# Key scores of a retention layer in three single-precision passes, placed inside the second product

## The reference, cut to what matters

```python
q = rotate_pairs(q, cos, sin)
k = rotate_pairs(k, cos, sin) * (dk ** -0.5)
scores = jnp.einsum('bhid,bhjd->bhij', qc, kc) * inner_decay[None]
inner = jnp.einsum('bhij,bhje->bhie', scores, vc)
out = out * lax.rsqrt(jnp.mean(out * out, axis=-1, keepdims=True) + RMS_EPS)
return (jax.nn.silu(g) * out) @ w_out
```

## Time and profile before

| | |
|---|---|
| median of 3 runs | 1968.48 us (1968.37 to 1968.97) |
| profiled execution | 1968.52 us |
| its span, first to last instruction | 1966.7 us |
| granted PE clock, mean | 0.999 of full speed |
| PE busy | 1943.1 us (99%) |
| DVE busy | 1464.6 us (74%) |
| ACT busy | 891.1 us (45%) |

### The profile page before, as it was taken

The page is one execution under the profiler, slowest core; times in us unless marked ns, Lnnn a source line. Parts: engine busy times, 40 slices in busy tenths (PEclk is TensorE's granted clock), DMA queues, the critical chain, the costliest instruction groups (busy, mean ns, idle before and its releaser), DMA issues.

```text
span 1966.7 us, 23704 instructions
## 1 busy us (share of the span) xinstructions
PE 1943.1 (99%) x9192; PEld 1618.4 (82%) x9192; DVE 1464.6 (74%) x1858; ACT 891.1 (45%) x1244; POOL 219.7 (11%) x163
## 2 busy tenths in 40 slices
PE   8999999999999999999999999999999999999998
PEld 7788888888888888888888888888897898888886
DVE  7999953886767859999843999983369769989722
ACT  5554632352524435545621554562168435554510
POOL 0000011100000031000021000002145440000121
PEclk9999999999999999999999999999999999999999
DMA  4233132331313320422232242223222014222331
GB/s 172 86 120 138 48 115 76 143 134 43 134 43 134 113 102 2 152 104 86 89 102 79 99 155 98 86 89 103 83 90 82 1 55 160 86 86 101 103 99 62
DMA packets 76189, 189.53 MB, mean 96 GB/s; under 512 B 4144, under 2 KB 12336, under 8 KB 73008
## 3 DMA queue, kind: packets, MB, share of 16 engines
q1 hardware_dynamic: 76080, 188.04, 27.4%
HBM read 185.92 MB, written 2.10 MB: 96 GB/s over the span
## 4 chain that ended last, share of the span: by engine, by line
PE 87%; DVE 8%; issue 2%; ACT 2%; SPq 0%; DMA 0%; POOL 0%; DVEq 0%; ACTq 0%
PE bank L2444 12%; PE bank L2446 12%; PE bank L2445 12%; PE bank L2436 12%; PE bank L2437 12%; PE bank L2438 12%; PE bank L2663 3%; PE bank L2665 3%; PE bank L2664 3%; PE bank L2544 2%; DVE part_lo L1560 1%; DVE idx_scores L2245 1%; DVE best L2241 1%; PE bank L2674 1%; PE bank L2920 1%
## 5 line engine op out<-in xcount | busy, mean ns | idle before, releaser
L1022 ACT ACTIVATE part_hi<-quad_w 128x1024 fp32r<-128x1024 f32 x280 | 293.1, 1064 | 279.0 <-PE bank L2446 192.5
L1560 DVE TENSOR_TENSOR part_lo<-quad_w,part_hi 128x1024 fp32r<-128x1024 f32 x280 | 330.5, 1221 | 26.4 <-ACT part_hi L1022 26.1
L2436 PE MATMUL bank<-gated_hi,out_hi 128*128 128x512 f32 x704 | 275.0, 391 | 0.0
L2437 PE MATMUL bank<-gated_lo,out_hi 128*128 128x512 f32 x704 | 274.3, 390 | 0.0
L2438 PE MATMUL bank<-gated_hi,out_lo 128*128 128x512 f32 x704 | 274.3, 390 | 0.0
L2444 PE MATMUL bank<-part_hi,s_hi 128*128 128x512 f32 x640 | 252.7, 395 | 3.0 <-DVE part_lo L1560 3.0
L2446 PE MATMUL bank<-part_hi,s_lo 128*128 128x512 f32 x640 | 249.7, 390 | 0.0
L2445 PE MATMUL bank<-part_lo,s_hi 128*128 128x512 f32 x640 | 249.5, 390 | 0.0
L2444 PE MATMUL bank<-part_hi,xn_hi 128*128 128x512 f32 x608 | 237.7, 391 | 2.5 <-DVE part_lo L1560 2.4
L2446 PE MATMUL bank<-part_hi,xn_lo 128*128 128x512 f32 x608 | 236.9, 390 | 0.0
L2445 PE MATMUL bank<-part_lo,xn_hi 128*128 128x512 f32 x608 | 236.9, 390 | 0.0
(11 more groups left out here) (306 smaller groups left out, 3548.9 us busy)
## 6 DMA issues: line engine op xcount, KB each, us to landing
quad_w<-w_ffn_in SPq DMA_DIRECT2D x80, 1024.0 KB, 7.4
out_raw<-w_ffn_out SPq DMA_DIRECT2D x64, 704.0 KB, 4.1
quad_w<-w_ret_in SPq DMA_DIRECT2D x14, 1024.0 KB, 7.4
rest_raw<-w_ffn_in SPq DMA_DIRECT2D x32, 256.0 KB, 5.2
quad_w<-w_ret_in SPq DMA_DIRECT2D x16, 512.0 KB, 5.0
quad_w<-w_ret_out SPq DMA_DIRECT2D x8, 1024.0 KB, 5.2
w_raw<-w_dsa SPq DMA_DIRECT2D x7, 1024.0 KB, 4.9
x_res<-x_in SPq DMA_DIRECT2D x8, 256.0 KB, 6.1
```

The source lines that it names most:

```text
L1022: nc.scalar.activation(in_four(part_hi[part_slot(h)]), source, copy).then_inc(part_hi_made, 1)
L1560: nc.vector.tensor_tensor(in_four(part_lo[part_slot(h)]), source, in_four(part_hi[part_slot(h)]).bitcast(FP32), ALU.subtract)\
L2436: mm(to, w_hi_of[:, at:at + width], hi, start=start, stop=False)
L2437: mm(to, w_hi_of[:, at:at + width], lo, start=False, stop=False)
```

## The change

The rotated query and key of each head are split too. ACT makes `q_hi` and `k_hi` and DVE `q_lo` and `k_lo` (each one instruction of 128x1024), and the key scores become three fp32r matmuls for each of the 8 before, 24 in all. They move from between products 0 and 1 to between the halves of product 1. `k_rot` and its remainder now lie where `p1` is, and `k_hi` where `u2` is, so ACT's copy of product 0 to `p1` waits until all the key scores of the head are done (`act.wait_ge(scores_done, BLOCKS * (h + 1))`).

```diff
-    k_rot = at("k_rot", post + 12288, 2 * SEQ)
+    q_lo = at("q_lo", post + 8192, 2 * SEQ, FP32R)
+    q_hi = at("q_hi", post + 12288, 2 * SEQ, FP32R)
+    k_rot = at("k_rot", post, 2 * SEQ)
+    k_lo = at("k_lo", post, 2 * SEQ, FP32R)
+    k_hi = at("k_hi", post + 4096, 2 * SEQ, FP32R)
...
+                def rotated_hi(h, kind):
+
+                    n = "qk".index(kind)
+                    act.wait_ge(qk_rotated, 2 * h + n + 1)
+                    nc.scalar.activation((q_hi, k_hi)[n][:, :], (q_rot, k_rot)[n][:, :], copy)\
+                        .then_inc(qk_hi_made, 1)
...
                         split_ret("o", h - 1, 2)
+                        rotated_hi(h, "q")
                         split_ret("o", h - 1, 3)
+                        rotated_hi(h, "k")
                         product_hi(h, 0)
                     else:
                         product_hi(h, 0)
                         turned_hi(h - 1)
                     product_hi(h, 1)
+                    if h in (0, RET_HEADS - 1):
+                        rotated_hi(h, "q")
+                        rotated_hi(h, "k")
+                    act.wait_ge(scores_done, BLOCKS * (h + 1))
                     copy_product(h, 0, p1, p1_copied)
                     product_hi(h, 2)
...
+                def rotated_lo(h, kind):
+
+                    n = "qk".index(kind)
+                    dve.wait_ge(qk_rotated, 2 * h + n + 1)
+                    dve.wait_ge(qk_hi_made, 2 * h + n + 1)
+                    nc.vector.tensor_tensor((q_lo, k_lo)[n][:, :], (q_rot, k_rot)[n][:, :],
+                                            (q_hi, k_hi)[n][:, :].bitcast(FP32), ALU.subtract).then_inc(qk_lo_made, 1)
...
                         update_head(h - 1, 6)
                         update_head(h - 1, 7)
-                        split_ret("g", h, 3)
                     else:
-                        product_lo(h, 1)
+                        split_ret("g", h, 2)
+                    rotated_lo(h, "q")
+                    rotated_lo(h, "k")
+                    split_ret("g", h, 3)
                     both_halves(h, 1)
                     decay_scores(h)
...
-                    pe.wait_ge(qk_rotated, 2 * h + 2)
+                    pe.wait_ge(qk_lo_made, 2 * h + 2)
                     for j in (0, 1, 3, 2):
                         for n in range(2):
-                            done = mm(scores_to(j), tile(k_rot, n * BLOCKS + j),
-                                      q_rot[:, n * SEQ + P * j:(n + 1) * SEQ], start=n == 0, stop=n == 1)
+                            of_k = tile(k_hi, n * BLOCKS + j), tile(k_lo, n * BLOCKS + j)
+                            of_q = slice(n * SEQ + P * j, (n + 1) * SEQ)
+                            mm(scores_to(j), of_k[0], q_hi[:, of_q], start=n == 0, stop=False)
+                            mm(scores_to(j), of_k[0], q_lo[:, of_q], start=False, stop=False)
+                            done = mm(scores_to(j), of_k[1], q_hi[:, of_q], start=False, stop=n == 1)
                         done.then_inc(scores_done, 1)
...
                     group_product(h, 0)
-                    key_scores(h)
                     if h == 0:
                         pe.wait_ge(s_lo_made, 7 * m + 1)
                     elif h < RET_HEADS - 1:
                         pe.wait_ge(head_updated, CHUNKS * h)
-                    group_product(h, 1)
+                    pe.wait_ge(qk_rotated, 2 * h + 1)
+                    group_product(h, 1, [0])
+                    key_scores(h)
+                    group_product(h, 1, [1])
                     pe.wait_ge(scores_decayed, BLOCKS * (h + 1))
```

More of the change, by code:

```diff
@@ L376, in build @@
     qk_rotated = sem("qk_rotated")
+    qk_hi_made, qk_lo_made = sem("qk_hi_made"), sem("qk_lo_made")
     v_scaled = sem("v_scaled")
@@ L2643, in left, with group_product @@
                     return tile(xn_hi, k * BLOCKS + t), tile(xn_lo, k * BLOCKS + t)
-                def group_product(h, i):
+                def group_product(h, i, halves=range(2)):
                     name = PRODUCTS[i]
                     to = {"x11w11": 0, "x12w21": 0, "S2T2": 2, "S3T3": 2, "x22T4": 2, "S1T1": 4, "S4w22": 4}[name]
-                    for half in range(2):
+                    for half in halves:
                         n = ret_part("g", h, 2 * i + half)
```

## The result

| | before | after |
|---|---|---|
| median of 8 runs each, on the same chip | 1969.21 us (1968.37 to 1970.13) | 1974.54 us (1973.49 to 1976.11) |
| profiled execution | 1968.52 us | 1974.42 us |
| its span | 1966.7 us | 1972.6 us |
| granted PE clock, mean | 0.999 | 0.999 |

The ratio is 1.0028, with a 95% interval of 1.0019 to 1.0036: slower by 5.3 us in the medians, by 3.7 to 7.1 us within the interval. The forecast was +4.4 us.

The account below looks back on a forecast made before the run. PE bounds the kernel, busy 99% of the span, with DVE a second engine without reserve in the first head. First head +3.06 and later heads +1.3 sum to +4.4 on 1968.5: 1972.9 us, own range 1972.0 to 1974.0.

Parts of the forecast that it names:

- rival 1: Key scores, all four heads: a 128-column matmul costs 0.218 us like the four-pass form; +7.0, 1975.5 us; chance 0.18.
- key scores, first to next start: 24 fp32r matmuls per head, six of each width, take 3.78 us, 0.58 less than before.
- E + 2.27: DVE's start on product 2's remainder, 2.27 us after E, when the next matmul could follow the key scores.
- wait in front of product 2, three later heads: PE waits 1.01 us: a 3.73 us chain is covered only by product 1's second half, 2.72.
- heads 2 to 4: From product 0's end to product 3, 15.67 us against 15.24: +0.43 each, +1.3 in all.
- first head, product 1: PE stands from 386.90 to 387.74 for product 1's first part, which the key scores covered before: +0.84 us.
- first head in all: DVE's lateness of 3.78 us after idle time makes product 6 and the head's results 3.06 us late.
- Rivals 1 and 2: Price of a 128-column matmul: 0.218 us (1975.5, chance 0.18), or 0.066 as loads don't bind it (1971.8, chance 0.14).
- Rival 3: Not slower: with 2.72 us instead of 3.73 it fits behind product 1's second half; -0.5, 1968.0 us; chance 0.08.
- the chain: After the key scores: ACT's two copies and rounded part, DVE's remainder, PE's restart before product 2; 3.73 us.
- rival 4: First head: DVE's debt isn't passed on, head costs 1.27, sum +2.6, 1971.1 us; chance 0.05.
- the 4.08: First head: DVE starts product 2's first remainder 4.08 us late (396.51 against 392.43).

Follow-up runs that it names:

- wait alone: Kernel before, with only ACT's copy of product 0 waiting for the fp32 key scores in their old place; 1969.92 us (one run).
- parts first: Changed kernel with ACT making product 2's parts before it waits and copies product 0; median 1970.09 us; also without the first head's two splits, 1969.21 us (one run).
- fp32 scores moved: Kernel before, its fp32 key scores moved between the halves of product 1, nothing split, no new wait; 1970.47 us beside 1971.10 (one run each).
- the same without splits: Changed kernel without DVE's two subtractions for query and key in the first head, rounded parts used instead; 1976.02 us (one run).
- fp32 moved, with the wait: Kernel before, fp32 key scores between the halves of product 1 and ACT's copy of product 0 waiting for them; 1976.28 us (one run).
- copies twice: Changed kernel with ACT's two copies of product 0 made a second time; 1983.31 us beside 1970.01 for the kernel before (one run each).
- the kernel with the narrow matmuls: Changed kernel with product 2's parts ahead of the copy, plus 32 unused fp32r matmuls of 64 to 256 columns in the last head; 1973.22 us (one run).

## Why the prediction was right

The forecast was slower by 4.4 us, with a place and a size for each part. The whole time alone doesn't decide between it and rival 1. The profiled execution, 1974.42, lies above the forecast's own range (1972.0 to 1974.0), 1.5 from 1972.9 and 1.1 from rival 1's 1975.5; the difference of the medians, +5.3, lies nearer to +4.4 than to rival 1's +7.0. What decides is the trace. The parts, in the prediction's order:

| step | predicted | measured |
|---|---|---|
| key scores, first to next start | 3.78 | 3.81, then 3.80, 3.80, 3.80 |
| six matmuls of 128 columns | 0.66 | 0.61 (490.25 to 490.86 below) |
| DVE's remainder behind the key scores | E + 2.27 | E + 2.26 |
| wait in front of product 2, three later heads | 1.01 | 15.72 - 14.70 = 1.02 |
| heads 2 to 4 | +0.43 each | +0.47, +0.48, +0.57 |
| first head, product 1 | +0.84 | 388.25 - 387.27 - 0.23 = 0.75, and 0.08 more behind it |
| first head in all | +3.06 | +3.02 |
| layer | +4.4 | +4.54 |

```profile
490.25 0.22 PE L2704 MATMUL bank<-q_hi,k_hi 128*128 128x128 f32 x1
...
490.86 0.33 PE L2704 MATMUL bank<-q_hi,k_hi 128*128 128x256 f32 x1
```

**The narrow matmul.** I took 0.11 from the distance of two weight loads, between bounds of 0.066 and 0.218. In the key scores six take 0.61 us, 0.10 each; the first of them is followed after 0.06, the others after 0.11, and the first matmul of 256 columns behind them is followed after 0.17 to 0.18 instead of 0.12. By itself it is 0.11. Rivals 1 and 2 fall. The rate of 55.8 ns for 128 columns (the Trainium skill, TensorE: Matmul & The Clock Gate, "Wait — 56ns, not 53.3ns?"), by which an estimate of the whole was 1970.8, isn't borne out by the fp32r matmuls of this trace: 0.10 to 0.11.

**The wait.** Rival 3, the chain fits behind 2.72 us, falls: the chain is 3.73. Lengthening it by 1.12 lengthened the second head by 1.12 (15.72 to 16.84), and taking it away gave 1.02 back. The move without the wait and the wait without the move cost the later heads nothing.

**The first head.** Right in size and in the way the debt travels, wrong in one reason. For the kernels with the DVE rows at hand, lateness of DVE's first remainder of product 2 (from the start of product 0; 10.98 before) less the two reserves, 0.30 on DVE and 0.72 in front of product 6, gives the loss:

| kernel | remainder starts at | late by | less 1.02 | first head |
|---|---|---|---|---|
| wait alone | 12.02 | 1.04 | 0.02 | +0.03 |
| parts first, with and without splits | 13.34, 13.34 | 2.36 | 1.34 | +1.25, +1.25 |
| fp32 scores moved | 13.91 | 2.93 | 1.91 | +1.84 |
| changed kernel | 15.08 | 4.10 | 3.08 | +3.02 |
| the same without splits | 15.07 | 4.09 | 3.07 | +2.99 |
| fp32 moved, with the wait | 15.58 | 4.60 | 3.58 | +3.53 |
| copies twice | 16.23 | 5.25 | 4.23 | +4.17 |

The loss follows the lateness within 0.1 over eight kernels besides the one before, so rival 4 (the debt isn't passed on) falls. But the prediction split the 4.08 into 2.27 for the two added splits and the rest for idle time. As a list of what DVE does in that time this holds; as a cause it is wrong: without the splits the lateness is the same 4.09, and without the chain it is 2.36 with them and without them. The two floors under DVE are the last decay, which needs the last key score, and the chain. The 1.25 that rival 3 worked out from the splits is what the kernel with the parts first shows, but by the decay: two floors happened to lie within 0.1 us of each other. I had reckoned one cause for the sum and not asked what stands there when it is taken away.

**Where 0.1 was missed.** The last head lost 0.57 for 0.43, and with the parts first it is 0.10 longer than the other heads. In it product 1's first part is ready only just in time (0.16 before product 0 ends by the row). I counted that as in time and left out that PE needs 0.15 from the end of a remainder to its start, and 0.08 behind it. In the changed kernel the second matmul of product 1 follows there after 0.29 instead of 0.23. But this can't be the whole cause: where the fp32 key scores were moved and nothing else, the remainder comes 0.16 before product 0 ends too, and product 1 starts without a loss (0.23). The changed list also has one wait more in front of product 1, for the rotated query; whether that makes the difference wasn't tried.

**The whole.** 1972.9 was forecast for the profiled execution, 1974.42 was measured. The layer explains 4.5 of 5.9; 0.61 lies ahead of the change, and the rest, 0.7 to 0.8, behind it, where the prediction had nothing; its cause is open.

## What to carry to other kernels

When work is moved past a producer, measure the distance from the new release to the first user, not the work: here the same wait was free behind 5.44 us of matmuls and cost 1.0 us in each head behind 2.72. In an in-order list a copy that nobody waits for soon can hold back the parts behind it that are needed next; one swap on ACT gave back 1.0 us in each later head. And before a delay is charged to added instructions, ask which other input of the late instruction comes at the same time.

## What the hardware showed that was not expected

**Narrow fp32r matmuls cost what their weight load costs.** 64, 128 and 192 columns all follow at 0.11 us, 256 at 0.12: from 256 to 128 columns a block of scores saves 0.01 us a matmul, and below 192 nothing more.

**A wait can cost a second time through the clock.** In the kernel with the copies made twice PE's wait in front of product 2 is 1.86 us instead of 0.74, in PE's timeline of the first head:

```profile
399.62 0.47 PE L2696 MATMUL bank<-part_hi,s_hi 128*128 128x512 f32 x1 [1.86 <-DVE part_lo L1596]
...
400.42 0.63 PE L2696 MATMUL bank<-part_hi,s_hi 128*128 128x512 f32 x1
400.84 0.63 PE L2697 MATMUL bank<-part_lo,s_hi 128*128 128x512 f32 x1
```

Behind it matmuls of 512 columns follow at 0.42 us instead of 0.23, the lower of the two clocks (1.2 GHz). The view by windows, stretches behind product 2's start in the four heads (columns: stretch, us, busy time of PE, PEld, DVE, ACT and POOL, granted clock, DMA share, GB/s):

```profile
399.60:404.00 4.40, 4.38 (x12) 3.48 (x13) 4.40 (x5) 4.40 (x8) 0.00 (x0) 0.61 0.00 0
497.40:503.00 5.60, 5.55 (x24) 4.61 (x25) 5.58 (x5) 4.57 (x6) 0.00 (x0) 1.00 0.00 0
593.60:600.80 7.20, 7.19 (x25) 5.79 (x26) 5.54 (x5) 4.64 (x6) 0.00 (x0) 0.76 0.00 1
669.60:676.80 7.20, 7.12 (x25) 5.75 (x25) 5.61 (x5) 4.71 (x6) 0.00 (x0) 0.76 0.01 2
```

And the changed kernel in the first head, behind a wait of 0.74:

```profile
398.50:404.20 5.70, 5.69 (x25) 4.45 (x25) 5.70 (x6) 5.70 (x10) 0.00 (x0) 1.00 0.00 0
```

All four are of one execution. Behind three of the four waits of 1.86 us the clock fell, behind one (the second head) it didn't. The length of the wait alone doesn't decide it elsewhere either: in the sparse attention layer every kernel here has a wait of PE of about 1.6 us; in the kernel with the narrow matmuls (wait before 1515.24) the granted clock is 0.50 from 1517.2 to 1520.4, and in the kernel before it is 1.00 at the same place. In the third and fourth heads this cost 1.60 and 1.67 us beyond the wait (18.44 and 18.51 against 16.84). In the first head product 2 takes 7.17 instead of 5.68 for the same reason, but there DVE's debt would have held PE up behind it anyway: nothing of it is left in the +4.17, for which DVE's lateness gives 4.23 alone. What tells the second head from the others was not tried.
